# Starting places of the activation buffers within 512 bytes, and single rows of 1/rms read twice

## The reference

```
h = rmsnorm(x) ; proj = h @ w_in                       # 1024 -> 5120
y_a = moba_attention(8 heads of 64) @ w_br_moba        # one block of 256: causal softmax with ALiBi
y_b = stick_breaking_attention(8 heads of 64) @ w_br_sb
x = x + (sigmoid(gate_a) * y_a + sigmoid(gate_b) * y_b) @ w_out
x = x + cross_attention(rmsnorm(x), rmsnorm(mem))      # 4 heads of 128, 256 memory tokens
x = x + square(relu(rmsnorm(x) @ w_up)) @ w_down       # 4096 wide
return rmsnorm(x)
```

## Time and profile before

| | |
|---|---|
| Time, median of 3 runs | 431.07 us (430.5 to 432.3) |
| Profiled execution, its own time | 431.82 us |
| Its span in the trace | 429.7 us |
| PE busy | 415.4 us, 2839 matmuls |
| Weight loads busy | 383.1 us |
| DVE busy | 339.7 us |
| ACT busy | 252.0 us |
| DMA | 77.47 MB, mean 180 GB/s |

### The profile page before, as it was taken

The page is one execution under the profiler, slowest core; times in us unless marked ns, Lnnn a source line. Parts: engine busy times, 40 slices in busy tenths (PEclk is TensorE's granted clock), DMA queues, the critical chain, the costliest instruction groups (busy, mean ns, idle before and its releaser), DMA issues.

```text
span 429.7 us, 7047 instructions
## 1 busy us (share of the span) xinstructions
PE 415.4 (97%) x2839; PEld 383.1 (89%) x2839; DVE 339.7 (79%) x444; ACT 252.0 (59%) x295; POOL 25.7 (6%) x39
## 2 busy tenths in 40 slices
PE   6999999999999999999999999999999999999991
PEld 6999988999999999889998898999999999999980
DVE  4669447877766544885846889999999999999985
ACT  5753335956736553460646568866666667777623
POOL 0069100000000000000010000000000000000002
PEclk9899999999999999999999999999999999999996
DMA  7999454525333444554534235555555555555002
GB/s 222 414 421 390 169 173 172 195 99 175 119 99 117 179 142 168 187 203 183 197 111 184 98 124 178 193 203 194 198 203 204 204 205 195 205 206 182 2 1 98
DMA packets 12971, 77.47 MB, mean 180 GB/s; under 512 B 1552, under 2 KB 2064, under 8 KB 4496
## 3 DMA queue, kind: packets, MB, share of 16 engines
q1 hardware_dynamic: 12800, 77.08, 49.2%
q10 hardware_dynamic: 144, 0.02, 0.0%
HBM read 76.04 MB, written 1.05 MB: 179 GB/s over the span
## 4 chain that ended last, share of the span: by engine, by line
PE 51%; DVE 24%; issue 15%; ACT 6%; DMA 1%; DVEq 0%; SPq 0%; POOLq 0%; POOL 0%; ACTq 0%
PE bank L1062 22%; PE bank L1081 13%; PE bank L1176 10%; DVE w_lo L646 5%; DVE t_lo L646 4%; DVE t_sum L901 4%; DVE t_sum L894 4%; DVE res L997 1%; PE bank L1188 1%; DMA xT_raw<-in_xT_dram 1%; ACT w_hi L405 1%; DVE forms L930 1%; DVE forms L935 1%; DVE forms L940 1%; PE bank L1274 1%
## 5 line engine op out<-in xcount | busy, mean ns | idle before, releaser
L646 DVE TENSOR_TENSOR w_lo<-raw,w_hi 128x2048 fp32r<-128x2048 f32 (+3 forms) x91 | 150.7, 1662 | 28.2 <-ACT w_hi L405 25.4
L1062 PE MATMUL bank<-hT_hi,w_hi 128*128 128x256 f32 x416 | 119.4, 287 | 2.9 <-DVE w_lo L646 2.3
L1062 PE MATMUL bank<-hT_lo,w_hi 128*128 128x256 f32 x416 | 118.6, 285 | 0.0
L1062 PE MATMUL bank<-hT_hi,w_lo 128*128 128x256 f32 x416 | 118.6, 285 | 0.0
L1062 PEld LDWEIGHTS bank<-hT_hi,w_hi 128*128 128x128 f32 x416 | 80.8, 194 | 4.4 <-issue 2.2
L1062 PEld LDWEIGHTS bank<-hT_lo,w_hi 128*128 128x128 f32 x416 | 80.8, 194 | 0.6
L1062 PEld LDWEIGHTS bank<-hT_hi,w_lo 128*128 128x128 f32 x416 | 80.7, 194 | 0.0
L405 ACT ACTIVATE w_hi<-raw 128x2048 fp32r<-128x2048 f32 x33 | 62.8, 1914 | 30.0 <-PE bank L1062 17.4
L1176 PE MATMUL bank<-hT_hi,w_hi 128*128 128x256 f32 x128 | 37.0, 289 | 0.2 <-DVE mem_row L689 0.2
L646 DVE TENSOR_TENSOR t_lo<-t_sum,t_hi 128x1024 fp32r<-128x1024 f32 x30 | 36.5, 1216 | 0.0
L1176 PE MATMUL bank<-hT_lo,w_hi 128*128 128x256 f32 x128 | 36.2, 283 | 0.0
(11 more groups left out here) (192 smaller groups left out, 820.5 us busy)
## 6 DMA issues: line engine op xcount, KB each, us to landing
raw<-in_weights_dram SPq DMA_DIRECT2D x65, 1024.0 KB, 4.8
raw<-in_weights_dram SPq DMA_DIRECT2D x7, 256.0 KB, 6.5
raw<-in_weights_dram SPq DMA_DIRECT2D x2, 512.0 KB, 8.0
res<-in_x_dram SPq DMA_DIRECT2D x2, 512.0 KB, 11.9
mem_tok<-in_mem_dram SPq DMA_DIRECT2D x1, 1024.0 KB, 9.6
memT_raw<-in_memT_dram SPq DMA_DIRECT2D x1, 1024.0 KB, 8.4
out_dram<-xs SPq DMA_DIRECT2D x2, 512.0 KB, 2.6
xT_raw<-in_xT_dram SPq DMA_DIRECT2D x3, 256.0 KB, 5.3
```

The lines of the kernel that those rows point to most:

```text
L646: return nc.vector.tensor_tensor(dst, whole, high.bitcast(fp32), sub)
L1062: last = mm(outs[m], w, v[:, k0 + k, :], start=first and n == 0, stop=k == nk - 1 and n == 2, skip_group_check=bool(kt_wait))
```

## The change

A helper `skip_to` moves the next buffer's start to a given place within 512 bytes. With it, and with fixed offsets for the buffers that lie over others, the starts within 512 bytes become:

| Buffer | before | after |
|---|---|---|
| raw, w_lo, w_hi, t_sum, t_lo, qkT, v_tok, gateT, xs | 128 | 128 |
| hT_hi / hT_lo | 128 / 128 | 256 / 320 |
| mT_hi / mT_lo | 128 / 128 | 384 / 416 |
| mixT_hi / mixT_lo | 128 / 128 | 0 / 64 |
| aT_hi / aT_lo, and over them f_hi / f_lo | 128 / 128 | 192 / 320 |
| t_hi | 128 | 320 |

`rstd_row` and `mem_row` shrink from 2048 to 1024 bytes of a partition each. They are written by one copy instead of two and read through an access pattern that goes over the same 256 columns twice.

```
+        def skip_to(place_in_512):
+            at[0] += (place_in_512 - at[0]) % 512
...
         res = sb("res", [P, TOK, D])
+        skip_to(256)
         hT_hi = sb("hT_hi", [P, KT, SEQ], f32r)
+        skip_to(320)
         hT_lo = sb("hT_lo", [P, KT, SEQ], f32r)
-        mT_hi, o = place("mT_hi", [P, KT, SEQ], f32r)
+        o = at[0]
+        skip_to(384)
+        mT_hi = sb("mT_hi", [P, KT, SEQ], f32r)
+        skip_to(416)
+        mT_lo = sb("mT_lo", [P, KT, SEQ], f32r)
         t_hi = sb("t_hi", [P, 2, 4 * 512], f32r, over=o)
-        mT_lo = sb("mT_lo", [P, KT, SEQ], f32r)
+        skip_to(128)
...
-        mixT_hi = sb("mixT_hi", [P, KT, SEQ], f32r, over=o)
-        mixT_lo = sb("mixT_lo", [P, KT, SEQ], f32r, over=o + 8192)
+        mixT_hi = sb("mixT_hi", [P, KT, SEQ], f32r, over=o + 384)
+        mixT_lo = sb("mixT_lo", [P, KT, SEQ], f32r, over=o + 8192 + 448)
+        at[0] += 512
...
+        skip_to(192)
         aT_hi, o = place("aT_hi", [P, 8, SEQ], f32r)
         f_hi = sb("f_hi", [P, 2, 8 * P], f32r, over=o)
+        skip_to(320)
         aT_lo, o = place("aT_lo", [P, 8, SEQ], f32r)
         f_lo = sb("f_lo", [P, 2, 8 * P], f32r, over=o)
+        skip_to(128)
...
-        rstd_row = sb("rstd_row", [P, 2, SEQ])
-        mem_row = sb("mem_row", [P, 2, SEQ])
+        rstd_row = sb("rstd_row", [P, SEQ])
+        mem_row = sb("mem_row", [P, SEQ])
...
             def spread(dst, b, rows):
                 dve.wait_ge(row_done, rows)
-                for j in range(2):
-                    last = nc.vector.tensor_copy(dst[:, j, :], bank[b][:, 0:SEQ])
-                last.then_inc(row_ready, 1)
+                nc.vector.tensor_copy(dst[:, :], bank[b][:, 0:SEQ]).then_inc(row_ready, 1)
+
+            def halves_of(t):
+                return t.rearrange("p (a n) -> p a n", a=2)
+
+            def twice(row):
+                return row.rearrange("p (a n) -> p a n", a=1).to_broadcast([P, 2, SEQ])
...
-                nc.vector.tensor_tensor(flat(gateT[:, 2 * h:2 * h + 2, :]), bank[h % 2][:, :],
-                                        flat(rstd_row[:, :, :]), ALU.mult).then_inc(gate_evac, 1)
+                nc.vector.tensor_tensor(gateT[:, 2 * h:2 * h + 2, :], halves_of(bank[h % 2][:, :]),
+                                        twice(rstd_row[:, :]), ALU.mult).then_inc(gate_evac, 1)
```

More of the change, by code:

```diff
@@ L710, in _ @@
                 dve.wait_ge(w_used, c + 1)
-                nc.vector.scalar_tensor_tensor(flat(qkT[:, 2 * c:2 * c + 2, :]), bank[c][:, :],
-                                               DH ** -0.5 if c % 4 < 2 else 1.0, flat(rstd_row[:, :, :]),
+                nc.vector.scalar_tensor_tensor(qkT[:, 2 * c:2 * c + 2, :], halves_of(bank[c][:, :]),
+                                               DH ** -0.5 if c % 4 < 2 else 1.0, twice(rstd_row[:, :]),
                                                ALU.mult, ALU.mult).then_inc(qk_evac, 1)
@@ L789, in mem_k_out @@
                 dve.wait_ge(w_used, MK[i] + 1)
-                nc.vector.tensor_tensor(flat(mkT[:, 2 * i:2 * i + 2, :]), bank[b][:, :], flat(mem_row[:, :, :]),
+                nc.vector.tensor_tensor(mkT[:, 2 * i:2 * i + 2, :], halves_of(bank[b][:, :]), twice(mem_row[:, :]),
                                         ALU.mult).then_inc(mk_evac, 1)
```

## The result

The changed kernel takes 433.35 us (median of 22 runs, 431.78 to 434.98) against 431.95 us for the kernel before on the same chips (22 runs, 430.4 to 433.24). The ratio is 1.0035, 95% interval 1.0021 to 1.0048: slower by about 1.5 us. The predicted range, 423 to 435 us, holds it, but the forecast was a gain of 0.3 us, and the interval leaves no room for a gain. The profiled execution has a span of 432.8 us and a time of 434.95 us.

What follows compares the result with a forecast made beforehand. PE was taken to bound most of the kernel, with DVE nearly level in the MLP. From 431.82 us, -0.3 for the copy and 0 for the other three terms gave 431.5, or 430.8 against the median; range 423 to 435.

Steps and rivals of the forecast that it cites:

- Copy: One copy less per row of 1/rms: 0 for `rstd_row`, -0.3 us for the awaited `mem_row`, bounds 0 to -0.35.
- Broadcast reads: Eighteen evacuations reading 1/rms through a pattern with a repeated half: no extra price, counted at 0.
- Other starts, seen by DVE and ACT: DVE and ACT working on buffers at new places, transfers unchanged: counted at 0.
- Other starts, seen by PE: PE's moving operand and next weight load starting 64 to 448 bytes apart: 0 ns per matmul, bounds on both sides.
- a fixed price of changing the weights at full rate: Reading of the 13.3 ns each fp32r matmul costs beyond its columns: other starts would not change it.
- The faster one passes the slower one: Load walks 512 bytes, moving operand 1024, so a shifted start moves their meeting and need not remove it: 0 ns.
- none is seen: DVE, ACT and POOL use SBUF at unrelated places, yet 210 PE matmuls take 25.00 us without scatter: against collisions.
- The load's duration as a measure: Weight loads take 186 ns alone, 192 beside 256 columns, 188 beside 512: collision priced at 6 or 2 ns.
- the second rival: PE's matmuls lose the load's stretch, 6 ns (256 columns) or 2 ns (512) each: 423 us, chance 20% including parts.
- The fourth rival: New starts collide in all PE stages, 6 or 2 ns more per matmul, MLP in full: 443.6 us, chance 15%.
- The double bound of the MLP: MLP step takes PE 10.540 us, DVE 10.508: faster PE meets DVE at once, slower PE sets the time.

Runs made afterwards that it cites:

- rows_only: Kernel before with only the single copy of 1/rms and the broadcast read, all buffers kept at 128 within 512 bytes: ratio 0.9989 (0.9971 to 1.0007).
- sweep1: Layer left out, 40 streams of 24 matmuls, activations' distance from weights in 32-byte steps: 113.8 to 120.0 ns (256 columns), 227.1 to 233.8 (512).
- sweep2: As sweep1 with 48 matmuls, finer steps, unequal high/low distances, last streams beside working DVE and ACT: 113.3 to 123.1 ns for 256 columns.

## Why the prediction was wrong

*Copy: right.* Forecast -0.3 us, measured -0.3 in `rows_only`, and the wait is gone at the forecast place.

*Broadcast reads: right.* The evacuations take 682 and 687 ns on average in both kernels, and `rows_only` shows no loss.

*Other starts, seen by DVE and ACT: right.* DVE's step stays at 10.508 us.

*Other starts, seen by PE: this is the step that failed.* It was priced at 0, as "a fixed price of changing the weights at full rate". The runs showed that the price is not fixed: it moves with the distance of the two starts, from 113.3 to 123.1 ns for 256 columns and from 227 to 234 for 512. Two of the arguments for 0 fell. "The faster one passes the slower one" was meant to make one distance much like another, and it does not. And "none is seen", the missing scatter beside other engines, showed only that other engines' traffic doesn't reach PE's reads. It was silent on PE's two reads against each other. The kernel before has no row in which the two starts differ, so its trace could not have shown the price. What the term should have been is +1.1 ns for most of the matmuls on `hT`, -2 to -3 for `aT` and `mT`, +6 ns for a 512-column matmul with `hT` or `mixT` stationary and about +3 in the down product. The bounds held the first two. For 512 columns they allowed a loss of 2 ns, and that bound was too small.

*The load's duration as a measure: wrong.* The loads do not follow the matmul's price. They went from 192 to 189 ns in q/k while the matmul went from 120.0 to 121.1, and they take 188 ns beside 512 columns, whether a matmul costs 227 or 233 ns. The 6 ns of the second rival are close to what the best distance gives back (120.0 to 113.3), but nothing ties the two, so the rival's size was luck. It also took for granted that moving the starts at all would give the gain. The changed kernel's distances for `hT`, 128 and 192, are a pair of the worse kind, though 192 alone is the best.

*The fourth rival* (slower because new starts cost more than equal ones, and the MLP counts in full, since PE is the later one) is the one whose direction came about. Its size did not: +1.5 us where it had +12.5, which is 0.6 ns for each of its 2547 matmuls. For `hT` it was a sixth of the 6 ns, for 512 columns three times the 2 ns, and `aT` and `mT` went the other way. So the direction of the sum is a balance of terms, which no part of the prediction had. Its chance of 15% was too low for a case in which no row had excluded the sign.

*The double bound of the MLP: right for the steady steps.* A slower PE cost 0.10 us in each at once. A faster one met DVE at 10.51. What it left out is DVE's one step of 11.03 us, by which a faster PE gains 0.03 us over the MLP and not 0.5.

Not shown is the mechanism inside: whether and how the two reads get in each other's way, what in them has a period of 256 bytes, and why q/k finds the slower rhythm at 192.

## What to carry to other kernels

- For a stream of fp32r matmuls, each with its own weight load, the distance modulo 256 bytes between the moving operand's start and the next load's start is a parameter worth a sweep: moved activations of 256 columns were best 192 bytes behind, moving weights of 512 columns best at 0. A one-launch sweep of 40 streams gives the table. Test each buffer in the role in which it is used, and don't let anything else, such as the PSUM bank, come round in step with the distance.
- When every operand in a trace has the same alignment, the trace says nothing about alignment. Give such a term a chance of both signs and let the bounds speak, above all where the engine concerned is the bound.

## What the runs showed of the hardware

- One matmul of 256 columns takes 113.3 to 123.1 ns in a steady stream by the distance of two starts (`sweep1`, `sweep2`), and a step of 4 bytes matters (113.3 at 192, 121.9 at 196).
- A stream settles into a repeating cycle, often of three or six matmuls, and more than one cycle can exist at one distance (117.8, 120.0 and 121 for the pair 128/192, 113.3 and 117.8 for 192). It then lasts for the whole stretch, 216 matmuls of q/k. What ran before seems to pick it.
- While the clock is at the lower level the distance doesn't show: the changed kernel's first matmuls there (pair 128/192) start 213.3 ns apart, as those at distance 0 of the kernel before do.
